# First two feed-forward units interleaved by token tile, squares moved behind them, and the loads and turns around the last state part put in another order

## The reference

```
x = x + 0.5 * swiglu(rms_norm(x, ln_ffn1), ffn1_gate, ffn1_up, ffn1_down)   # 2816 hidden features
y, state, shift, va = token_mix(rms_norm(x, ln_mix), ...)                   # chunked gMLP and RWKV-7, side by side
x = x + y
x = x + cross_attn(rms_norm(x, ln_xattn), mem_k, mem_v, xa_q, xa_o)         # 256 memory tokens, 4 heads
x = x + 0.5 * swiglu(rms_norm(x, ln_ffn2), ffn2_gate, ffn2_up, ffn2_down)
...
mem_k, mem_v = (rms_norm(mem, mem_norm) @ xa_k), (rms_norm(mem, mem_norm) @ xa_v)   # prompt group
S_t = S_{t-1} diag(w_t) + (S_{t-1} (-kk_t)) (kk_t * a_t)^T + v_t k_t^T ;  o_t = S_t r_t   # RWKV-7
o = group_norm(o) + bonus;  yb = o * g
```

## Time and profile before

| | |
|---|---|
| median of 3 runs | 2682.27 us (2677.46 to 2686.69) |
| the profiled execution, its own time | 2681.58 us |
| its span from the first to the last instruction | 2679.8 us |
| TensorE busy | 2569.7 us, 96% |
| VectorE, GpSimd, ScalarE busy | 1089.4, 1095.2, 537.8 us |
| mean granted TensorE clock | 0.981 of full speed |
| moved by DMA | 158.02 MB, 59 GB/s over the span |

### The profile page before, as it was taken

How to read it: one execution, slowest core, us unless ns; L and a number is a source line. 1 busy time by engine, 2 the same in 40 slices (tenths; PEclk the granted TensorE clock), 3 DMA queues, 4 the chain that set the end, 5 groups by cost and what they waited for, 6 DMA issues and landing times.

```text
span 2679.8 us, 50157 instructions
## 1 busy us (share of the span) xinstructions
PE 2569.7 (96%) x20493; PEld 2479.7 (93%) x20493; DVE 1089.4 (41%) x1846; ACT 537.8 (20%) x1114; POOL 1095.2 (41%) x867
## 2 busy tenths in 40 slices
PE   5999999999999999799998999889999999999997
PEld 4999999999999998688887799879999999999997
DVE  6332133213362375555663653364533223322323
ACT  4110011001130212634334420132211001100102
POOL 3444444444454343122223754105444444444442
PEclk7999999999999999999998999999999999999999
DMA  3111111111123111000022513262111111111112
GB/s 115 46 44 47 47 47 47 47 44 46 39 71 111 38 44 56 1 4 4 21 71 89 185 48 104 76 219 65 47 44 46 47 47 47 47 47 44 46 39 75
DMA packets 222439, 158.02 MB, mean 59 GB/s; under 512 B 11016, under 2 KB 211298, under 8 KB 221419
## 3 DMA queue, kind: packets, MB, share of 16 engines
q1 hardware_dynamic: 219114, 140.11, 17.4%
q10 hardware_dynamic: 2720, 16.09, 1.5%
q0 software_dynamic: 480, 0.05, 0.0%
HBM read 141.09 MB, written 15.12 MB: 58 GB/s over the span
## 4 chain that ended last, share of the span: by engine, by line
PE 90%; DVE 4%; issue 3%; ACT 2%; DMA 1%; SPq 0%; POOL 0%; DVEq 0%; ACTq 0%; POOLq 0%
PE bank L411 26%; PE bank L413 26%; PE bank L412 26%; PE bank L1073 1%; PE bank L1101 1%; PE bank L1088 1%; DVE s_junk L2092 1%; PE bank L1117 1%; PE bank L1121 1%; PE bank L1048 1%; PE bank L1142 1%; PE bank L1155 1%; PE bank L1132 0%; PE bank L1144 0%; PE bank L886 0%
## 5 line engine op out<-in xcount | busy, mean ns | idle before, releaser
L381 POOL TENSOR_TENSOR w_hi<-raw,cst 128x512 fp32r<-128x512 f32 (+1 forms) x366 | 463.9, 1268 | 1209.1 <-PE bank L413 1072.1
L411 PE MATMUL bank<-h_hi,w_lo 128*128 128x344 f32 (+1 forms) x2856 | 915.8, 321 | 7.5 <-issue 7.5
L413 PE MATMUL bank<-h_hi,w_hi 128*128 128x344 f32 (+1 forms) x2856 | 913.1, 320 | 0.0
L412 PE MATMUL bank<-h_lo,w_hi 128*128 128x344 f32 (+1 forms) x2856 | 912.7, 320 | 0.0
L411 PEld LDWEIGHTS bank<-h_hi,w_lo 128*128 128x128 f32 (+1 forms) x2856 | 535.9, 188 | 9.8 <-issue 7.6
L413 PEld LDWEIGHTS bank<-h_hi,w_hi 128*128 128x128 f32 (+1 forms) x2856 | 536.1, 188 | 1.2
L412 PEld LDWEIGHTS bank<-h_lo,w_hi 128*128 128x128 f32 (+1 forms) x2856 | 535.1, 187 | 1.8
L386 POOL TENSOR_TENSOR w_lo<-raw,w_hi 128x512 fp32r<-128x512 f32 (+1 forms) x386 | 504.3, 1307 | 53.0 <-ACT w_hi L378 24.1
L413 PE MATMUL bank<-hid_hi,w_hi 128*128 128x344 f32 x1056 | 337.3, 319 | 0.0
L411 PE MATMUL bank<-hid_hi,w_lo 128*128 128x344 f32 x1056 | 337.2, 319 | 0.0
L412 PE MATMUL bank<-hid_lo,w_hi 128*128 128x344 f32 x1056 | 337.1, 319 | 0.0
(11 more groups left out here) (318 smaller groups left out, 3024.9 us busy)
## 6 DMA issues: line engine op xcount, KB each, us to landing
raw<-in_ffn_gate SPq DMA_DIRECT2D x88, 256.0 KB, 2.8
raw<-in_ffn_up SPq DMA_DIRECT2D x88, 256.0 KB, 2.9
raw<-in_ffn_down SPq DMA_DIRECT2D x80, 256.0 KB, 2.8
raw<-in_w_in SPq DMA_DIRECT2D x44, 256.0 KB, 2.8
cache<-in_cache_mem_k SPq DMA_DIRECT2D x8, 1024.0 KB, 5.1
cache<-in_cache_mem_v SPq DMA_DIRECT2D x8, 1024.0 KB, 5.1
x_save<-x ACTq DMA_DIRECT2D x1, 4128.0 KB, 12.5
x<-x_save ACTq DMA_DIRECT2D x8, 516.0 KB, 7.7
```

The lines of the kernel that those rows point to most:

```text
L381: nc.gpsimd.tensor_tensor(w_hi[part], raw[part], cst[:, C_ONE:C_ONE + 1, 0:ph["width"]].to_broadcast([P, nk, ph["width"]]), ALU.mult)\
L411: nc.tensor.matmul(out, b, hi, start=first, stop=False)
L412: nc.tensor.matmul(out, a, lo, start=False, stop=False)
L413: m = nc.tensor.matmul(out, a, hi, start=False, stop=last)
```

## The change

**At the start.** SyncE loads only the first two tables, then the weights of unit 0, blocks 0 to 2, the weights of unit 1, blocks 3 to 7, the sample tokens and the other ten tables. TensorE turns six blocks, then does tile 0 of unit 0 and of unit 1, then turns blocks 6 and 7 and the sample tokens into other banks, then tile 1 of both units, then tile 2 of both. ScalarE makes a tile's eight high parts in a row, and its squares only after the high parts of the next tile; VectorE makes the low parts in a row and adds the squares one tile later. The sums over partitions, roots and reciprocals come tile by tile.

**Around the last state part.** `x_tensor(7, 0)` goes ahead of `mem_tensor`; ScalarE's `mem_scalar` is no longer cut in two by `x_scalar(7, 0)`; `u_scalar(7, 1)` goes ahead of `unit_high(4)`; `act_slot(4)` and `out_scalar(7, 1)` go ahead of `unit_high(5)`. SyncE issues `unit_load(2)` ahead of the wait for the sample rows, and `unit_load(4)` and `(5)` ahead of the wait for the bonus. The turn of the sample rows moves from slot 3 to slot 5, into unused columns of another bank.

```diff
-        def pairs(eng, ph, step, static=False):
-            first = 0
+        def pairs(eng, ph, step, static=False, skip=0):
+            first = skip
...
                 pe.wait_ge(evac[st], i * nt + ph["mm0"][st])
+                if only is not None:
+                    for h, (slot, turn), (k0, nk) in pieces:
                         pe.wait_ge(split_done[slot], turn + 1)
+                        product(h, slot, k0, nk, only)
                     return
...
-            mem_tensor(pe)
             x_tensor(pe, 7, 0)
+            mem_tensor(pe)
             out_state_tensor(pe, 7, 0)
...
-            mem_scalar(act, 0, 4)
             x_scalar(act, 7, 0)
-            mem_scalar(act, 4, 8)
+            mem_scalar(act, 0, KD)
             u_scalar(act, 7, 0)
             unit_high(act, 2)
             out_scalar(act, 7, 0)
             unit_high(act, 3)
             x_scalar(act, 7, 1)
+            u_scalar(act, 7, 1)
             unit_high(act, 4)
-            u_scalar(act, 7, 1)
             act_slot(act, 4)
+            out_scalar(act, 7, 1)
             unit_high(act, 5)
-            out_scalar(act, 7, 1)
...
+            unit_load(sp, 2)
             sp.wait_ge(S("smp_in"), 96)
             sp.dma_start(smp_on[:, :], smp_od).then_inc(S("smp_in"), 16)
-            unit_load(sp, 2)
             unit_load(sp, 3)
+            unit_load(sp, 4)
+            unit_load(sp, 5)
             sp.wait_ge(S("bo2"), 4)
             sp.dma_start(ya_in[:, :, :], y_save).then_inc(S("ya_in"), 16)
-            unit_load(sp, 4)
-            unit_load(sp, 5)
             sp.wait_ge(S("smp_t"), 7)
...
         @block.sync
-            sp.dma_start(cst[:], A["constants"]).then_inc(S("cst_in"), 16)
-            sp.dma_start(xnat_s[0:NS, :], A["x_sample"][:, 0, :]).then_inc(S("x_in1"), 16)
+            sp.dma_start(cst[:, 0:C_BLK, :], A["constants"][:, 0:C_BLK, :]).then_inc(S("cst_in"), 16)
+            one_unit(ffn1[0][0], load_body(sp, ffn1[0][0]), 0)
             for n in range(8):
                 sp.dma_start(xnat[:, n, :], A["x_prompt"][0, n * P:(n + 1) * P, :])\
...
+                if n == 2:
+                    one_unit(ffn1[0][0], load_body(sp, ffn1[0][0]), 1)
...
         @block.tensor
+            for t in range(3):
+                if t == 0:
+                    pe.wait_ge(S("xt_a"), 6)
+                    pe.wait_ge(S("xt_b"), 6)
+                pe.wait_ge(S("x_lo"), KD * (t + 1))
+                for u in (0, 1):
+                    one_unit(ffn1[0][0], first, u, only=t)
+                if t == 0:
+                    pe.wait_ge(S("fin_in"), 48)
+                    turn_x(6, 6, 7)
+                    turn_x(7, 2, 5)
...
+                if t == 1:
+                    rms_sum(pe, 0, 0, KD)
+            rms_sum(pe, 0, 1, 2 * KD)
+            rms_sum(pe, 0, 2, 3 * KD)
+            pe.wait_ge(S("cst_in"), 32)
             for a, b in ffn1:
                 if a["f0"] == 0:
-                    multiply(pe, a, tile_ready=lambda t: pe.wait_ge(S("x_lo"), KD * (t + 1)),
-                             after_first=lambda: rms_tensor(pe, 0))
+                    multiply(pe, a, skip=1)
...
         @block.scalar
+            evict_x(0)
+            high_x(0)
+            evict_x(1)
+            high_x(1)
+            square_x(0)
+            evict_x(2)
+            high_x(2)
+            square_x(1)
+            rms_root(act, 0, 0)
+            square_x(2)
+            rms_root(act, 0, 1)
+            rms_root(act, 0, 2)
...
         @block.vector
+            for t in range(3):
+                evict_x(t)
...
-                for k in range(KD):
-                    split_vector(dve, 0, "ln_ffn1", h_hi, h_lo, k, t, KD * t + k)
-            rms_vector(dve, 0)
+                low_x(t)
+                if t > 0:
+                    acc_x(t - 1)
+            rms_inverse(dve, 0, 0)
+            acc_x(2)
+            rms_inverse(dve, 0, 1)
+            rms_inverse(dve, 0, 2)
+            dve.wait_ge(S("cst_in"), 32)
```

More of the change, by code:

```diff
@@ L322, in pairs @@
                 return
-            if ph["u0"] == 0 or "peel" in ph:
+            if not skip and (ph["u0"] == 0 or "peel" in ph):
                 step(0)
@@ L337, in run @@
                     after(2 * i + s)
-            pairs(eng, ph, lambda i: [run(i, s) for s in (0, 1)], static=after is not None)
+            pairs(eng, ph, lambda i: [run(i, s) for s in (0, 1)], static=after is not None, skip=skip)
             if ph["units"] % 2:
@@ L341, in unit_steps, with one_unit @@
                 run(i, 0)
-        def one_unit(ph, body, u):
+        def one_unit(ph, body, u, **part):
             i, s = u // 2, u % 2
-            body(i, s, [((2 * (ph["u0"] + s) + h) % 4, (2 * (ph["u0"] + s) + h) // 4 + i) for h in (0, 1)])
+            body(i, s, [((2 * (ph["u0"] + s) + h) % 4, (2 * (ph["u0"] + s) + h) // 4 + i) for h in (0, 1)],
+                 **part)
         def split_k(kt):
@@ L397, in multiply_body, with body @@
             low_of = ph["lo"] if isinstance(ph["lo"], list) else None
-            def body(i, s, turns):
+            def body(i, s, turns, only=None):
                 st = (ph["u0"] + s) % 2
@@ L2297, in _, with turn_x @@
             pe.wait_ge(S("cst_in"), 16)
-            for n in range(8):
-                pe.wait_ge(*((S("x_in0"), 16) if n < 1 else (S("x_in1"), 64) if n < 4 else (S("x_in2"), 64)))
-                b = 2 * (n % 4)
+            def turn_x(n, lo, hi):
+                for k in range(KD):
+                    m = nc.tensor.transpose(bank[lo if k < 4 else hi][:, (k % 4) * P:(k % 4 + 1) * P],
+                                            xnat[:, n, k * P:(k + 1) * P], ident)
+                    if k % 4 == 3:
+                        m.then_inc(S("xt"), 1)
+            first = multiply_body(pe, ffn1[0][0])
+            for n in range(6):
+                pe.wait_ge(*((S("x_in0"), 16) if n < 1 else (S("x_in1"), 32) if n < 3 else (S("x_in2"), 48)))
                 if n >= 4:
@@ L2384, in _, with square_x @@
                 for k in range(KD):
-                    split_scalar(act, 0, "ln_ffn1", h_hi, k, t, KD * t + k)
-            rms_scalar(act, 0)
+                    high_scalar(act, "ln_ffn1", h_hi, k, t)
+            def square_x(t):
+                for k in range(KD):
+                    square_acc_scalar(act, 0, k, t, KD * t + k)
+            act.wait_ge(S("const"), 4)
+            evict_x(0)
[10 more added lines that the diff above has]
+            rms_root(act, 0, 2)
             prev = None
@@ L2414, in _, with evict_x, low_x, acc_x @@
             nc.vector.memset(vnat[:, :], 0.0).then_inc(S("vz"), 1)
-            for t in range(3):
+            def evict_x(t):
                 for n in range(3 * t, min(3 * t + 3, 8)):
                     dve.wait_ge(S("xt"), 2 * n + 2)
+                    b = (1, 3, 5, 7, 1, 3, 7, 5)[n]
                     nc.vector.tensor_copy(x[:, 4:8, n * P:(n + 1) * P],
-                                          bank[2 * (n % 4) + 1][:, :].rearrange("p (k n) -> p k n", k=4))\
+                                          bank[b][:, :].rearrange("p (k n) -> p k n", k=4))\
                         .then_inc(S("xt_b"), 1)
+            def low_x(t):
+                for k in range(KD):
+                    low_vector(dve, 0, "ln_ffn1", h_hi, h_lo, k, t, KD * t + k)
+            def acc_x(t):
+                for k in range(KD):
+                    acc_vector(dve, 0, k, t, KD * t + k)
+            for t in range(3):
+                evict_x(t)
                 if t == 0:
```

100 lines of the change are left out of this document (56 added, 44 removed).

## The result

The changed kernel takes 2663.42 us (median of 4 runs, 2662.14 to 2666.9); the kernel before took 2682.59 us beside it on the same chip. The ratio is 0.9932, with an interval of 0.9912 to 0.9951: 19 us faster, between 13 and 24. Forecast were 2665.5 us and a gain of 16.

What follows compares the result with a forecast made beforehand. PE (TensorE) was taken to bound the kernel, by its waits and lower clock level. Last state part 14 plus start 2 gave 16 off 2681.6: 2665.6, stated as 2665.5 us; own range 2661 to 2669, wider range 2655 to 2675.

Steps and rivals of the forecast that it cites:

- I start at the lower level for the 5.9 us that it lasted before: Tile 0 of units 0 and 1: 20 matmuls at the lower clock, 28 at 0.157 us, 10.3 us, ending at 35.8.
- The first rival: Start: GpSimd's splits do not hold up tile 2's eight sums; 6 us more gain, 2659.5 us; chance 0.17.
- The second rival: Start: turns of blocks 6 and 7 lose the clock, tile 1 begins at half level; +2.7, 2668 us; chance 0.08.
- (b): Last state part: units 4 and 5 load earlier, so PE's 5.0 us wait for `Us` goes whole.
- (c): Last state part: without that gap the clock need not fall at 1432 us; 12.37 us at half level become 6.2.
- (d): Last state part: the 2.7 us wait for `nkk` stays and may lower the clock; half a chance of 2.4, -1.2.
- (a): Last state part: `x_tensor(7, 0)` fills the 2.56 us wait for memory tokens; unit 0 begins 2.8 us earlier (2.5 to 3.2).
- unit 0's half level: Last state part: unit 0's 3.5 us at half clock may go as well; 0.8 us, half of what it could give.
- (e): Last state part: the moved turn of the sample rows costs the same; its new wait is covered by unit 5.
- The third: Start: gain vectors or blocks land later, the chain of sums takes the rest; -3 to -5, 2671 us; chance 0.09.
- The fourth: Last state part: the wait at `Us` only moves and half level stays; 2673 to 2676 us, no change; chance 0.11.
- The fifth: Between units 4 and 15: idle gaps keep PE at the lower clock, slower; at 60 us of it 2696 us; chance 0.05.

Runs made afterwards that it cites:

- e1: The kernel before with only the change's edits of the start: 2677.55 us, ratio 0.9984.
- e3: The changed kernel, but GpSimd splits the weights of units 2 and 3 only after the last sum of squares: 2662.18 us, ratio 0.9929.
- e4: The changed kernel, but VectorE's three small `aux` instructions stand behind the evictions of blocks 3 to 5: 2663.69 us, one run.
- e2: The kernel before with only the edits of the last state part, the sample turn and the loads: 2667.87 us, ratio 0.9948.
- e5: The kernel before with one edit, ScalarE's `u_scalar(7, 1)` ahead of `unit_high(4)`: 2673.05 us, one run.
- e6: The kernel before with one edit, the loads of units 4 and 5 ahead of SyncE's wait for the bonus: 2671.61 us, one run.
- e10: The changed kernel itself, measured once more: 2665.78 us, ratio 0.9934.
- e7: The kernel before with one edit, `x_tensor(7, 0)` ahead of the memory tokens, whose ScalarE copies are no longer cut in two: 2673.54 us, one run.

## Why the prediction was right, and where it was off

**The time and its direction** came out as forecast: 2663.42 against 2665.5, inside the forecast's own range. The sum of 16 stands against 16.3 by the means of the table and 19 (13 to 24) by the runs. That it came so close by the means is in part luck: the start gave 1.5 more than forecast and the last state part 0.8 less, and inside that part one term was twice too large (below). What the 3 us between table and runs are is not settled; they lie within what untouched code varies.

**The start: +2 forecast, 3.5 by the table, 4.8 (1.6 to 7.0) by e1.** The mechanism was right step by step: first split 9.34 (forecast 9.3), first product 25.39 (25.5), eight sums 10.5 us long (10.6), PE idle from about 53 to 66. The step that was mis-sized is "I start at the lower level for the 5.9 us that it lasted before". In the first tile it lasted until 28.3 us, 2.9 us, so the tile ended at 34.4 instead of 35.8; in unit 2 it lasted 3.3 us, which costs about 1.6 instead of 2.7. Blocks 6 and 7 with the sample took 2.8 us instead of 3.2. The first and the last of these made the start of unit 2 1.6 us early (66.2 against 67.8); the shorter lower level there adds another 1.1 at unit 2's end.

**Sums held up by the splits.** The first rival, that they are not, is refuted: e3 shows 4.6 us without splits and after shows 10.5 with them. The rival's price, 6 us at unit 2, was about right (5.4), but a shorter idle time does not come back whole.

**The small `aux` instructions.** The row had shown alternation for two operands only. The Trainium skill's page "SBUF — State Buffer", section "Who interferes with whom", says that `tensor_scalar` can take the shared ports as well; the trace agrees (1.04 and 1.20 us beside splits, 0.16 and 0.17 without, e4). The low parts ended at 23.5 us, which was forecast without this, by two errors that cancelled: the small instructions took 2.4 us together, but GpSimd's splits took 1.28 us each instead of up to 1.5, and ended at 19.7 instead of 20.5, so that fewer low parts had to take turns with them.

**Transposes and the clock.** The second rival is refuted for the turns that it names. Those of blocks 6 and 7 took 0.12 us each, the granted clock from 34.6 to 38 us was 1.00, and tile 1 began at full level. The Trainium skill's page "TensorE: Matmul & The Clock Gate", section "Part 4: PE-mode transpose", says that transposes do not count as busy in the same way; the trace does not show the level fall behind these 2.8 us of turns (1.00). It did fall under earlier ones: behind a wait of 2.25 us the 24 turns of blocks 3 to 5 took 4.48 us (granted clock 0.50 from 18.5 to 21 us), and in e3 2.81 us at 1.00. No run separates that wait from the turning as the cause, and nothing waited for those turns.

**The last state part: 13.6 forecast, 13.7 between the two profiles, 12.8 by the means, 14.5 (9.7 to 18.5) by e2.** Terms (b), (c) and (d) came to 5.0 + 6.2 - 1.2 = 10.0; measured 9.9 and 10.3. The wait ahead of the last state's turn stayed (2.3 us, now for VectorE's new state, for 2.7) and dropped the clock, as (d) had it at half a chance. Terms (a) and unit 0's half level came to 3.6; measured 3.8 against before's profile and 2.5 by the means. The sum fits, its two terms don't. Where unit 0 begins, in before, in e1 (old order) and after:

```profile
1407.38 0.39 PE L411 MATMUL bank<-mem_hi,alt_lo 128*128 128x256 f32 x1 [1.55 <-DVE mem_lo L1692]
1401.57 0.58 PE L410 MATMUL bank<-mem_hi,alt_lo 128*128 128x256 f32 x1 [1.55 <-DVE mem_lo L1706]
1399.82 0.39 PE L410 MATMUL bank<-mem_hi,alt_lo 128*128 128x256 f32 x1 [2.91 <-DVE mem_lo L1705]
```

Counted from the table load, that is 38.82 us in before, 36.41 to 36.42 in e1, e5 and e6, which have the same order, and 34.99 to 35.01 in all eight profiles with the edit. So the order is worth 1.4 us and not the 2.8 of (a): the 2.56 us wait for the memory tokens goes, but the wait for their last low part grows from 1.55 to 2.91 us, which (a) did not have. The other 2.4 us are before's own execution, in which the 16 turns of the memory tokens took 3.65 us at the lower level (granted clock 0.50 from 1396 to 1400 us); in e1, e5 and e6 they took 1.94 us behind the same wait. The 0.8 for unit 0's half level did not come: it lasts 3.3 us after the change (1400.7 to 1404) for 3.5 before. The 2.5 of the means holds some luck of the clock as well, since from unit 0's begin to the bonus e1, e5 and e6 took 10.4 to 11.9 us, and the profiles with the edit 10.65 to 10.68. Term (e), the sample turn, shows in no wait.

**The other rivals.** The third, a lost start, and the fourth, a wait that only moves, are refuted by e1 and by the waits after the change. The fifth, a lower level that lasts, by the clock of 1.00 from 1432 to 1440 us and by the last column, which does not change.

## What to carry to other kernels

When a start is brought forward, ask what VectorE must still do once TensorE has used up the early work, and which engine takes turns with it then: here 13 to 15 of 18 us were given back to a chain of sums and roots that earlier had been covered. A wait of TensorE can cost more than its length: behind 2.3 us of it the clock fell here, and the price was 4.1. Compare kernels by the distance between instructions that both have, over several profiles, before a microsecond is given to an edit: untouched stretches here differed by 6 us.

## What the runs showed of the hardware that was not expected

- The same code behind the same wait ran at the lower clock level for different lengths: in unit 2 some 3.3 us in one profile of the changed kernel, and in e10 still partly after 69.5 us (0.50 from 66 to 69.5 us, 0.75 from 69.5 to 73). An earlier start of unit 2 (e3) met 6.2 us of it.
- Where the level falls in untouched code differs too: from the start's end to the last state part 1269.5 to 1276.0 us over twelve profiles. Added up from the granted clock of stretches of 4 us, the lower level held for some 14 us of it in e7, the shortest, and for some 31 in e2, e3, e5 and e6, the longest; half of that difference is 8.5 us, which covers the 6.4 between the shortest and the longest. With `x_tensor` first, the stretch from the table load to the bonus took 45.64 to 45.68 us in eight profiles; with the old order, where PE waits 2.56 us in it, 46.8 to 49.5 in four.
- A `tensor_scalar` over 4 columns took 1.20 us beside a split of GpSimd and 0.17 us without; reciprocals of 128x344 took 2.2 to 2.3 us either way.
